# The first norm after the flip instead of before it, and the local attention's counts as logarithms in its mask

## The reference

```python
def rms_norm(x, g):
    y = x * lax.rsqrt(jnp.mean(x * x, axis=-1, keepdims=True) + EPS)
    return y * g

h = x
for l in range(DEPTH):
    y = hybrid_mixer(rms_norm(h, mix_norm_pre[l]), positions, w_in[l], ...)
    h = h + rms_norm(y, mix_norm_post[l])
    ...
```

## Time and profile before

| | |
|---|---|
| median of 3 runs | 817.45 us (816.84 to 817.47) |
| the profiled execution | 817.97 us, its span 815.8 us |
| busy: TensorE / VectorE / ScalarE / POOL | 807.4 / 653.9 / 528.3 / 29.3 us |
| read from HBM | 143.87 MB, 178 GB/s over the span |

### The profile page before, as it was taken

The page is one execution under the profiler, slowest core; times in us unless marked ns, Lnnn a source line. Parts: engine busy times, 40 slices in busy tenths (PEclk is TensorE's granted clock), DMA queues, the critical chain, the costliest instruction groups (busy, mean ns, idle before and its releaser), DMA issues.

```text
span 815.8 us, 12147 instructions
## 1 busy us (share of the span) xinstructions
PE 807.4 (99%) x4636; PEld 698.2 (86%) x4636; DVE 653.9 (80%) x1149; ACT 528.3 (65%) x823; POOL 29.3 (4%) x54
## 2 busy tenths in 40 slices
PE   8999999999999999999999999999999999999997
PEld 5998888889888888888899889888998888888885
DVE  6899996778776899997387999948788489999753
ACT  5656886567657777765365589756767477776441
POOL 2100000010010000000010000001000000000000
PEclk9999999999999999999999999999999999999999
DMA  8765345472574465556666453456635545655651
GB/s 300 285 180 182 96 137 168 143 258 95 168 242 141 157 205 204 179 187 218 193 205 231 151 155 104 136 175 204 209 114 196 181 130 181 202 174 191 231 182 52
DMA packets 40446, 145.72 MB, mean 179 GB/s; under 512 B 4594, under 2 KB 4738, under 8 KB 40388
## 3 DMA queue, kind: packets, MB, share of 16 engines
q1 hardware_dynamic: 38448, 138.38, 52.1%
q0 software_dynamic: 1936, 6.55, 2.3%
q10 hardware_dynamic: 4, 0.00, 0.0%
HBM read 143.87 MB, written 1.05 MB: 178 GB/s over the span
## 4 chain that ended last, share of the span: by engine, by line
PE 96%; DVE 2%; issue 1%; ACT 1%; DMA 0%; DVEq 0%; POOLq 0%; POOL 0%; ACTq 0%
PE acc L1685 8%; PE acc L1651 5%; PE acc L1652 5%; PE acc L1653 5%; PE psCD L1685 4%; PE acc L1695 4%; PE acc L1668 4%; PE acc L1748 4%; PE psAB L1685 4%; PE acc L1750 4%; PE acc L1749 4%; PE acc L1669 3%; PE acc L1670 3%; PE psAB L1651 3%; PE psAB L1652 3%; PE psAB L1653 3%
## 5 line engine op out<-in xcount | busy, mean ns | idle before, releaser
L996 DVE TENSOR_TENSOR wlo<-raw,whi 128x1024 fp32r<-128x1024 f32 x240 | 288.0, 1222 | 68.3 <-ACT whi L569 66.7
L569 ACT ACTIVATE whi<-raw 128x1024 fp32r<-128x1024 f32 x240 | 249.7, 1058 | 119.4 <-PE acc L1653 43.6
L1685 PE MATMUL acc<-xT,whi 128*128 128x512 f32 x288 | 89.0, 390 | 0.0
L1685 PEld LDWEIGHTS acc<-xT,whi 128*128 128x128 f32 x288 | 54.1, 188 | 11.8
L1539 DVE SCALAR_TENSOR_TENSOR KT<-V,par,KT 128x255 f32<-128x255 f32 (+1 forms) x144 | 60.0, 480 | 2.1 <-ACT KT L929 1.5
L1695 PE MATMUL acc<-xT,wlo 128*128 128x256 f32 x288 | 58.0, 283 | 0.0
L1276 DVE SCALAR_TENSOR_TENSOR arena<-arena,par 128x256 f32<-128x256 f32 x120 | 50.3, 482 | 0.8 <-ACT arena L769 0.8
L1668 PE MATMUL acc<-xT,whi 128*128 128x256 f32 x176 | 50.9, 289 | 0.0
L1685 PE MATMUL psCD<-xT,whi 128*128 128x512 f32 x160 | 50.0, 393 | 0.0
L1669 PE MATMUL acc<-xT,whi 128*128 128x256 f32 x176 | 49.7, 283 | 0.0
L1670 PE MATMUL acc<-xT,wlo 128*128 128x256 f32 x176 | 49.7, 282 | 0.0
(11 more groups left out here) (336 smaller groups left out, 2084.0 us busy)
## 6 DMA issues: line engine op xcount, KB each, us to landing
raw<-stream_dram SPq DMA_DIRECT2D x256, 512.0 KB, 4.2
gpost<-gain_dram POOLq DMA_DIRECT2D x6, 512.0 KB, 5.2
gpre<-gain_dram POOLq DMA_DIRECT2D x5, 512.0 KB, 5.9
memn<-mem_dram SPq DMA_DIRECT2D x2, 512.0 KB, 10.0
out_dram<-h SPq DMA_DIRECT2D x4, 256.0 KB, 2.1
cst<-const_dram SPq DMA_DIRECT2D x1, 896.0 KB, 6.3
h<-x_dram SPq DMA_DIRECT2D x2, 256.0 KB, 3.0
h<-x_dram SPq DMA_DIRECT2D x1, 512.0 KB, 7.4
```

Source lines behind the costliest of these rows:

```text
L569: act.activation(home(g)[0], raw[:, s * GW:(s + 1) * GW], ACT.Copy).then_inc(w_hi.sem, 1)
L996: dve.tensor_tensor(lo, raw[:, cols], hi.bitcast(F32), ALU.subtract).then_inc(w_lo.sem, 1)
L1685: e = pe.matmul(up_halves(j, c), whi[:, cols], both, start=k == 0, stop=k == KC - 1)
```

## The change

In layer 0, for the first norm:

- TensorE flips x as it arrives. The gain is brought onto the partitions as 8 columns (one small matmul, one copy) and is applied as the scale of the copies out of PSUM: four instructions of 128 columns for each high part (ScalarE) and each low part (VectorE) where there was one of 512. The first flip goes by halves into two banks; VectorE does the second half's high part.
- The root of each token is applied behind the projections: for q and k of C in the cosines and sines (`trig0`), for v of C and v of A as the scale of a copy, for the columns of B by a row of roots (`root_row`) that two matmuls of ones by a diagonal spread, in two more operations on VectorE, for q of A by that row and for k of A as the scale in the mask. The squares, sums and roots of x move behind those of the memory, between the splits of groups 4 to 7.
- The transfers: constants and gain on ScalarE's queue at once, weight group 0 between the halves of x; POOL's load of the cross attention's gain waits until the last reader of the row of roots and the angles is through, as they lie in its buffer. The parameters' load follows the roots of x.
- `first_pass` takes groups 0 and 1 for both token halves first and signs them off sooner.
- Six idle products before and four after the first flip.

The angles are worked out in two parts in the opening, and their sine is taken there.

In the local attention of both layers the counts no longer multiply: `log_counts`, once, in layer 0 ahead of the first scores, adds their logarithms (times 8, as the scores are scaled later) to the mask; ScalarE's exponential gives the sums with `accum_out`; of each pair VectorE scales the second head and ScalarE the first.

```diff
-            for n in range(2):
-                sp_.dma_start(h[:, n * NT:(n + 1) * NT], x[0:P, n * NT:(n + 1) * NT]).then_inc(x0_in[n].sem, 16)
-            sp_.dma_start(cst[:, 0:CC_TRI], consts[:, 0:CC_TRI]).then_inc(head_in.sem, 16)
+            first_rows(0)
             group(0)
+            first_rows(1)
             group(1)
...
-            before_sub_layer(0, 0, 0)
             pool.dma_start(posi[:, :], pos).then_inc(pos_in.sem, 16)
-            before_sub_layer(0, 0, 1)
...
+            for t in range(TOK):
+                before_sub_layer(0, 0, t)
             load_params(0)
...
-                pool.wait_ge(xn_ready.sem, xn_ready.at(l, 2 * TOK))
+                if l:
+                    pool.wait_ge(xn_ready.sem, xn_ready.at(l, 2 * TOK))
+                else:
+                    pool.wait_ge(root_row_in.sem, 1)
+                    pool.wait_ge(gpad_in.sem, 1)
+                    pool.wait_ge(k_roped.sem, TOK)
+                    pool.wait_ge(sbT_in.sem, 2)
                 gain(gpre, gpre_in, l, X_PRE)
...
+            def first_input_hi(t, b, n=4):
+                act.wait_ge(gain0_cols.sem, 1)
+                act.wait_ge(x0_tr.sem, 1)
+                if t or b:
+                    act.wait_ge(xt_tr.sem, 2 * t + b + 1)
+                for c in range(n):
+                    e = act.activation(x_chunks(0, b, t)[:, c], first_block(t, b, c), ACT.Copy,
+                                       scale=gain0[:, 4 * b + c:4 * b + c + 1])
+                e.then_inc(xt_hi.sem, 1)
...
-            squares_x(0)
+            first_input_hi(0, 0, 2)
             split_group(0, 0)
-            for b in range(2):
-                first_input_hi(0, b)
             split_group(0, 1)
-            squares_x(1)
+            first_input_hi(0, 1)
+            first_input_hi(1, 0)
             split_group(0, 2)
             split_group(0, 3)
-            for b in range(2):
-                first_input_hi(1, b)
+            first_input_hi(1, 1)
+            act.wait_ge(trig_arg.sem, 1)
+            act.activation(trig[:, :], trig[:, :], ACT.Sin).then_inc(trig_ready.sem, 1)
...
-                            e = act.activation(p, p, ACT.Exp, bias=st(S_NB + 4 * (c % 2) + 2 * r + q),
-                                               scale=HD ** -0.5)
+                            e = act.activation(p, p, ACT.Exp, bias=st(S_NB + n), scale=HD ** -0.5,
+                                               accum_out=st(S_DEN + n))
...
-            norm_input(0, 0, 0)
-            for n in range(2):
-                first_scale(0, n)
+            first_input_rest()
+            first_input_lo(0, 0)
             split_group(0, 0)
-            first_input_lo(0, 0)
+            angles_first()
             split_group(0, 1)
-            norm_input(0, 0, 1)
             first_input_lo(0, 1)
-            for n in range(2):
-                first_scale(1, n)
+            first_input_lo(1, 0)
+            angles_rest()
             split_group(0, 2)
             split_group(0, 3)
-            for b in range(2):
-                first_input_lo(1, b)
+            first_input_lo(1, 1)
...
+                def log_counts():
+
+                    two, three = float(HD ** 0.5 * np.log(2.0)), float(HD ** 0.5 * np.log(3.0))
+                    bend = three / 2 - two
+                    rise = sms[1][0]
+                    own.link(dve.tensor_scalar(rise, mult, bend, two - 2 * bend, ALU.mult, ALU.add))
+                    own.link(dve.scalar_tensor_tensor(rise, mult, -1.0, rise, ALU.add, ALU.mult))
+                    own.link(dve.tensor_tensor(negm, negm, rise, ALU.add))
+
                 def probabilities(c):
 
                     w = 4 * (c % 2)
                     for r in range(2):
                         dve.wait_ge(exp_done.sem, exp_done.at(l, 2 * c + r + 1))
-                        for q, (a, b) in enumerate(((0, P), (P, AW))):
-                            p = sms[c % 2][r][:, a:b]
-                            e = dve.tensor_tensor_reduce(p, p, mult[:, a:b], 1.0, 0.0, ALU.mult, ALU.add,
-                                                         st(S_DEN + w + 2 * r + q))
-                        own.link(e)
                         dve.reciprocal(st(S_RDEN + w + 2 * r, 2), st(S_DEN + w + 2 * r, 2)).then_inc(den_ready.sem, 1)
+                    dve.wait_ge(den_ready.sem, den_ready.at(l, 2 * c + 2))
+                    for q, (a, b) in enumerate(((0, P), (P, AW))):
+                        p = sms[c % 2][1][:, a:b]
+                        e = dve.tensor_scalar(p, p, st(S_RDEN + w + 2 + q), None, ALU.mult)
+                    e.then_inc(p1_ready.sem, 1)
...
+                else:
+                    dve.wait_ge(root_row_in.sem, 1)
+                    dve.wait_ge(w_used.sem, w_used.at(l, g_cv + PER_TILE))
+                    dve.tensor_tensor(by_half(sig), by_half(accs[1][1][:, :]), by_token(2), ALU.mult).then_inc(gate_scaled.sem, 1)
+                    own.link(dve.tensor_tensor(gated_rows, by_half(accs[1][0][:, :]), by_token(2), ALU.mult))
+                    dve.wait_ge(cv_sig.sem, cv_sig.at(l, 1))
+                    dve.tensor_tensor(gated_rows, gated_rows, by_half(sig), ALU.mult).then_inc(gpad_in.sem, 1)
...
                 dve.wait_ge(cst_in.sem, 16)
+                if not l:
+                    log_counts()
                 scores_max(0)
...
-            idle_products(4)
-            pe.wait_ge(spread_set.sem, 1)
-            pe.wait_ge(gain0_in.sem, 16)
-            for n in range(2):
-                pe.matmul(psAB[n], pick[:, n * P:(n + 1) * P], gain0, start=True,
-                          stop=True).then_inc(gain0_spread.sem, 1)
-            pe.wait_ge(head_in.sem, 16)
-            first_input(0)
-            idle_products(2)
-            first_input(1)
+            idle_products(6)
+            pe.wait_ge(head_in.sem, 16)
+            pe.wait_ge(gain0_in.sem, 16)
+            pe.matmul(psAB[0][:, 0:KC], gain_rows, ident[0:KC, 0:KC], start=True, stop=True).then_inc(gain0_tr.sem, 1)
+            first_input(0, 0)
+            idle_products(4)
...
                     first_memory(1)
+                    spread_roots()
                     transposed_product(g_cv + 2, 2, X, acc[1], k0=4)
+                    pe.wait_ge(root_row_in.sem, 1)
```

More of the change, by code:

```diff
@@ L743, in _ @@
                         squares_memory(t, landed)
-                    split(g_cv + PER_TILE - 1)
+                        split(g_cv + t)
+                    for t in range(TOK):
+                        squares_x(t)
+                        split(g_cv + 2 + t)
                     memory_base(0)
@@ L808, in _ @@
                 act.wait_ge(w_used.sem, w_used.at(l, G_SBV + PER_TILE // 2))
-                act.activation(sbv, accs[1][0][:, :], ACT.Copy).then_inc(sbv_in.sem, 1)
+                for t in range(TOK):
+                    rows_t = slice(t * SB_W, (t + 1) * SB_W)
+                    e = act.activation(sbv[:, rows_t], accs[1][0][:, rows_t], ACT.Copy, scale=1.0 if l else st(S_HRS + t))
+                e.then_inc(sbv_in.sem, 1)
                 split(G_WK1 + AHEAD)
@@ new lines, in first_input_lo, with roots_diagonal, first_angles_scaled @@
+                e.then_inc(xt_lo.sem, 1)
+            def roots_diagonal(t):
+                dve.wait_ge(head_in.sem, 16)
+                dve.wait_ge(h_rs.sem, t + 1)
+                dve.tensor_scalar(diag[:, t * P:(t + 1) * P], ident, st(S_HRS + t), None,
+                                  ALU.mult).then_inc(diag_set.sem, 1)
+            def first_angles_scaled():
+                dve.wait_ge(trig_ready.sem, 1)
+                for t in range(TOK):
+                    cols = slice(2 * t * HALF, 2 * (t + 1) * HALF)
+                    own.link(dve.tensor_scalar(trig0[:, cols], trig[:, cols], st(S_HRS + t), None, ALU.mult))
@@ L1321, in _ @@
                         mean_square(S_MMS + t, S_YSQ + t).then_inc(mem_ms.sem, 1)
-                    memory_scale(0)
-                    split(g_cv)
-                    memory_scale(1)
-                    split(g_cv + PER_TILE - 1)
+                        split(g_cv + t)
+                        memory_scale(t)
+                    for t in range(TOK):
+                        norm_input(0, 0, t)
+                        split(g_cv + 2 + t)
+                    for t in range(TOK):
+                        roots_diagonal(t)
+                    own.link(dve.tensor_scalar(st(S_KRS, TOK), st(S_HRS, TOK), HD ** -0.5, None, ALU.mult))
                     dve.wait_ge(mem_gains_tr.sem, 1)
@@ L1857, in first_pass @@
                         pe.wait_ge((xt_hi if hi_x else xt_lo).sem, 2 * t + g // 2 + 1)
+                        if g == 1 and not t:
+                            pe.wait_ge(x0_hi_rest.sem, 1)
                         w, a0 = (whi if hi_w else wlo), (0 if hi_x else SEQ) + t * P
```

190 lines of the change are left out of this document (125 added, 65 removed).

## The result

The changed kernel took 820.09 us in the median of 16 executions (817.61 to 821.2), the kernel before 817.7 us (816.84 to 818.37, 16 executions) beside it: a ratio of 1.0022, interval 1.0015 to 1.0029. That is 2.4 us slower by the medians. The prediction said 816.3 us, 815.0 to 818.6.

What follows compares the result with a forecast made beforehand. TensorE, busy 99% of the span, was taken as the bound. The opening's 2.4 us lead, at most 2.7 with slack at k's rotation, less 1.6 for log_counts, keeps 1.1: 816.3 us against 817.45, range 815.0 to 818.6.

Steps and rivals of the forecast that it cites:

- Group 0 at 5.8 us, first weight matmul at 7.0: Opening: weight group 0 lands at 5.8 us instead of 7.97; first weight matmul starts at 7.0 us instead of 9.95.
- Rival (b): Opening: group 0 lands no sooner than 7.1 us, only 0.4 us kept, 817.0 us; chance 0.15.
- The clock up at about 9 us: Opening: TensorE reaches its fast matmul spacing at about 9 us, costing 0.2 us.
- rival (c): Opening: the clock rises later than before, as flips may count as a pause; 818.5 us; chance 0.2 in its late form.
- Second tile 12.6, product done 20.8, memory product 35.1: Opening to convolution: TensorE's wait for the second tile, first product's end and memory product's start, the last 2.4 us ahead.
- The last gate operation at 36.7 us: Layer 0's gate: VectorE's last operation stands at 36.7 us instead of 40.89.
- VectorE is 4.2 us ahead: VectorE's lead at the last gate operation; 3.7 us after the scaled angles, at most 2.7 us from k's rotation on.
- log_counts 1.6 us: Three linked VectorE operations ahead of layer 0's first local scores cost 1.6 us, leaving 1.1 us of the 2.7 us lead.
- ScalarE's accumulator reads: Local attention: ScalarE gains four accumulator reads of 0.1 us each per pair of heads, while losing two copies (0.7 us).
- A pause of 1.3 us on TensorE: Sign in the profile after: TensorE idles 1.3 us ahead of layer 0's second pair of local scores, none in layer 1.
- No new waits later: After the local scores nothing is late next; a new wait between 77 and 136 us would prove the forecast wrong.

Runs made afterwards that it cites:

- e4: Changed kernel plus seven unread 512-column matmuls on TensorE ahead of layer 0's second pair of local scores, filling its pause; 818.17 us.
- e1: Changed kernel without ScalarE's wait for the convolution product's end ahead of layer 0's gate sigmoid; 817.47 us, ratio 1.0004 to the kernel before.
- e12: Changed kernel with the local attention of the kernel before and one wait ahead of the sigmoid; 815.59 us against 817.21, ratio 0.9981.
- e5: Kernel before with only the attention's part of the change, opening and flips as before; 819.01 us against 817.5, ratio 1.0019.
- e6: Changed kernel with the local attention of the kernel before, late table load included; 816.66 us against 817.5, ratio 0.9992.
- e2: Changed kernel with log_counts moved into VectorE's wait for layer 0's sigmoid, table load still late; 816.9 us, ratio 0.9997.
- e3: Changed kernel with one wait ahead of the sigmoid and log_counts moved ahead of the last gate operation; 816.94 us, ratio 0.9996.
- e8: Changed kernel with one wait ahead of the sigmoid and log_counts on GpSimd behind the gate; 816.99 us against 817.5, ratio 0.9996.
- e11: Changed kernel with one wait ahead of the sigmoid, log_counts as one ScalarE Square and one VectorE operation before the last gate operation; 816.1 us against 817.21.
- e10: Changed kernel with the first two of log_counts' three operations done twice, lengthening TensorE's pause; six executions, 818.85 to 822.36 us.
- e13: Changed kernel with one wait ahead of the sigmoid and log_counts on GpSimd as soon as the constants land; 818.13 us against 817.21, ratio 1.001.

## Why the prediction was wrong

In short: two terms of the sum failed. VectorE's last gate operation was put at 36.7 us and stood at 39.31, so that its lead at the rotation of k was 1.07 us and not 2.7. And TensorE's pause ahead of the second pair of scores was priced at its own length, while the clock fell after it in nine of sixteen executions. With the first alone the time is that of the group that kept its clock, 818.24 us: no gain any more, but still within the range given. The second takes it out of the range. It would have been there with the lead of the prediction too, which had a pause of 1.3 us in it.

**Group 0 at 5.8 us, first weight matmul at 7.0.** Right in kind: ScalarE starts on group 0 at 6.27 us without waiting for its transfer, and the first weight matmul is at 7.56 us, 2.4 us sooner than before where 2.95 was said. Rival (b) did not come about. The largest gain in that term was reckoned wrongly, though: 5.1 us is 3.7 us and 512 KB at 392 GB/s; with the 768 KB that are named it is 5.7.

**The clock up at about 9 us, rival (c) if late.** The fast spacing is there from 9.5 us in the changed kernel's profile. The rise differs between executions, though: with the very same opening, the four idle products took 1.17 us in e4 and 2.05 us in the changed kernel, that is, the fast level came some 5 us sooner there (and gained 0.7 us at the first weight matmul, 6.85 us, as that then waits for its weights):

```profile
5.08 1.17 PE L1727 MATMUL acc<-idle 128*128 128x512 f32 x4
```
```profile
5.71 2.05 PE L1727 MATMUL acc<-idle 128*128 128x512 f32 x4
```

By the rule of the Trainium skill that the prediction weighed ("TensorE: Matmul & The Clock Gate", section Part 4: PE-mode transpose), the flips would be a pause and the rise late. No profile here shows the slow spacing after 10.7 us, and the opening never cost what rival (c) charges. Rival (c) had the clock as a danger in the wrong place.

**Second tile 12.6, product done 20.8, memory product 35.1.** 13.01, 21.49 and 35.64 us: 0.4 to 0.7 us late, a lead of 1.8 us at the memory product instead of 2.4. Sizes, not mechanisms.

**The last gate operation at 36.7 us: the first step that failed.** It was at 39.31 us, 2.6 us later. Half a microsecond of that is TensorE's own lateness at the memory product. Two terms were missing besides. First, VectorE's own queue: from 27.5 to 37.7 us it runs without a gap, so the first gate operation stands at 36.52 us behind VectorE's work and not behind TensorE's product; the memory's and x's roots on GpSimd took about 1.45 us each where the kernel before had 0.56 and 0.99 for the memory's, and VectorE waited 1.2 us for them. Second, the sigmoid's table load: 1.28 us, hidden before only in part (the earlier trace rows stood behind sine, load and sigmoid) and here behind VectorE's scaling. e1 takes the second term away and the operation moves up by 1.3 us against its own queue; the first stays, in e12 too (37.90 us). So "VectorE is 4.2 us ahead" was 1.6 us at the gate and 1.07 us at the rotation, not 2.7.

**log_counts 1.6 us.** Exact: 0.35, 0.56 and 0.56 us and the links, 73.71 to 75.31 us. So was the way it was charged: lead less 1.6 us. With the true lead it is 1.07 - 1.60 = -0.53 us, and the executions in which the clock stays up have 818.24 us against 817.7, 0.5 us. e5, e6 and e12 show the terms apart: the attention's part costs 1.5 us where no lead pays for it (1.35 without the two executions at 0.997), the opening brings 0.8 us with the late load and 1.6 us without it. Of the small terms, ScalarE's accumulator reads were put at 0.1 us and took 0.19; they are on no path that decides.

**A pause of 1.3 us on TensorE, priced at its own length: the second step that failed.** It was 1.5 us, and I named it among the signs of the forecast without asking what it does to the clock, though the opening's rows had just shown idleness and clock together. 14 of 22 executions of the changed kernel have the lower mean clock; none of 22 of e1 (a pause of 0.4 us) and e4 (filled). This term, 2.1 us between the groups of executions and 1.6 us in the traces, was not in the sum and makes most of the 2.4 us. That the medians show it at all hangs on the share: with the fall in fewer than half of the sixteen executions the median would have been one of the other group.

**No new waits later.** Right for the changed kernel. In e2 and e3, which are further ahead, TensorE waits 0.4 us for VectorE in the query product near 167 us.

One more thing of method: the sum was made against an execution of 817.97 us. The kernel before spread over 816.1 to 818.4 us in all its executions, so that one lies near the long end, and gains read from two profiles (1.3 us for e8) came out larger than those of the medians (0.5 us). That bears on e1, e2, e3, e8, e11 and e12, all of which I expected 0.3 to 1.2 us too fast against the kernel before. The traces take it apart. At the product behind the second pair of scores (77.58 us in the kernel before) the profiled e12 is 2.07 us ahead, e8 1.69, e11 1.34, e6 1.18 and e1 0.10; at the last matmul (809.88 us) it is 1.99, 1.63, 1.39, 1.03 and 0.08. So nothing behind the scores takes the lead back but the 0.4 us of e2 and e3, and much of what is missing in the medians is the chosen execution, which lies 0.5 to 0.8 us above the medians of the kernel before on the three chips.

## What to carry to other kernels

Where an instruction that needs another function table gets a second wait, look at where the load stands: one wait fewer made it run 2.3 us earlier (2.9 against VectorE's gate operation) and moved the whole queue behind it by 1.3 us. Before a new wait is put on TensorE, price the clock as well as the wait: 1.5 us of idleness cost 1.6 to 2.1 us more in two executions of three. And when a lead is worked out for an engine's stage, sum its own queue up to there, not only the stage that feeds it.

## What was not expected of the hardware

- The table load took over a wait: with two waits ahead of an ACTIVATE that needs a new table, one stood on the load (1.28 us) and held it back, with one it did not. The Trainium skill ("ScalarE: Activation LUTs", section What ACT_TABLE_LOAD costs) has 1.28 us for the load and a drain of 1.38 us besides; the load agrees, a drain does not show: the sigmoid starts 1.29 us after the load does.
- The granted clock fell to 0.50 from 77.5 to 80.9 us, after a pause of 1.5 us that ended at 76.31, in some executions of a kernel and not in others. It stayed up through a pause of 2.4 us in e10 and through one of 1.4 us, which ended at 37.3 us, in e13.
- In e8 and e13 GpSimd and VectorE lengthened each other's fp32 operations on SBUF by a factor of up to three: GpSimd's tensor_scalar of 384 columns took from 0.51 to 1.57 us, VectorE's subtraction of 256 columns 0.42 us and 1.07 beside GpSimd.
